# Moved time tables and two-part norm factors in a two-block transformer kernel

## The reference

```python
# block 1, gated linear attention: 4 heads, chunks of 64
log_a = log_sigmoid(g_lr @ w_gate2 + b_gate) / 16
b = cumsum(log_a)                       # inside a chunk
q_t, k_t = q * exp(b), k * exp(-b)
o = tril(q_t @ k_t.T) @ v + q_t @ state # state: a scan over kd = k * exp(b_last - b)
# block 1, compressed attention: 8 heads, the keys pooled into blocks
probs = softmax(mask(q @ k_cmp.T))
h = h + concat([o_nsa, o_gla]) @ w_out  # "half output": o_gla's half of w_out
# block 2
proj = rmsnorm(h) @ w_in
q, k = l2norm(silu(conv(dq))), l2norm(silu(conv(dk)))   # 8 heads of 128
g = -exp(a_log) * softplus(da + dt_bias)
beta = sigmoid(db)
o_dn = gated_delta_rule(q, k, v, g, beta)               # scan over chunks of 64
o_dn = rmsnorm(o_dn, dn_gain) * silu(dz)
qs, ks = rmsnorm(sq, sbq_gain), rmsnorm(sk, sbk_gain)   # stick-breaking attention
merged = sigmoid(gate_dn) * (o_dn @ w_dn) + sigmoid(gate_sb) * (o_sb @ w_sb)
```

## Time and profile before

| | before |
|---|---|
| median of 3 runs | 2299.69 us (2299.67 to 2304.11) |
| the profiled execution | 2297.21 us |
| its span | 2295.4 us |
| TensorE busy | 2198.8 us, 96% of the span |
| TensorE weight loads | 1700.5 us |
| VectorE busy | 1119.2 us, 49% |
| ScalarE busy | 804.2 us, 35% |
| DMA | 218.65 MB, mean 95 GB/s |

### The profile page before, as it was taken

How to read it: one execution, slowest core, us unless ns; L and a number is a source line. 1 busy time by engine, 2 the same in 40 slices (tenths; PEclk the granted TensorE clock), 3 DMA queues, 4 the chain that set the end, 5 groups by cost and what they waited for, 6 DMA issues and landing times. The chain is left out here.

```text
span 2295.4 us, 32701 instructions
## 1 busy us (share of the span) xinstructions
PE 2198.8 (96%) x13572; PEld 1700.5 (74%) x13572; DVE 1119.2 (49%) x1800; ACT 804.2 (35%) x1310; POOL 67.4 (3%) x88
## 2 busy tenths in 40 slices
PE   8999799999999899989998999998999999999999
PEld 7776456888888888977665888666566578888887
DVE  3464675777733467654345443346432254444422
ACT  3333554444422443422224222225345433222221
POOL 0000001000000000000000000000012101000000
PEclk8999899999999999989999999999999999999999
DMA  4124001322222244321114321114721322222322
GB/s 162 63 74 149 8 1 65 98 96 92 93 99 93 89 146 136 112 97 64 63 56 160 133 91 64 60 57 166 239 67 49 115 101 92 92 92 92 101 92 92
DMA packets 78595, 218.65 MB, mean 95 GB/s; under 512 B 8688, under 2 KB 13168, under 8 KB 78448
## 3 DMA queue, kind: packets, MB, share of 16 engines
q1 hardware_dynamic: 78448, 216.57, 28.1%
HBM read 185.74 MB, written 29.75 MB: 94 GB/s over the span
## 5 line engine op out<-in xcount | busy, mean ns | idle before, releaser
L296 PE MATMUL ps<-nx_hi,whi 128*128 128x264 f32 (+1 forms) x1504 | 538.1, 358 | 17.5 <-DVE nx_lo L385 9.7
L274 ACT ACTIVATE whi<-raw 128x1024 fp32r<-128x1024 f32 x282 | 298.4, 1058 | 625.4 <-PE ps L298 446.7
L281 DVE TENSOR_TENSOR wlo<-raw,whi 128x1024 fp32r<-128x1024 f32 x282 | 346.6, 1229 | 345.3 <-ACT whi L274 344.6
L298 PE MATMUL ps<-nx_hi,wlo 128*128 128x264 f32 (+1 forms) x1504 | 512.4, 341 | 0.0
L297 PE MATMUL ps<-nx_lo,whi 128*128 128x264 f32 (+1 forms) x1504 | 511.9, 340 | 0.0
L296 PEld LDWEIGHTS ps<-nx_hi,whi 128*128 128x128 f32 x1504 | 286.4, 190 | 85.0 <-issue 37.2
L298 PEld LDWEIGHTS ps<-nx_hi,wlo 128*128 128x128 f32 x1504 | 286.6, 191 | 32.6
L297 PEld LDWEIGHTS ps<-nx_lo,whi 128*128 128x128 f32 x1504 | 287.0, 191 | 30.4 <-issue 1.9
L298 PE MATMUL ps<-x_hi,wlo 128*128 128x512 f32 x528 | 209.6, 397 | 0.0
L297 PE MATMUL ps<-x_lo,whi 128*128 128x512 f32 x528 | 208.3, 395 | 0.0
L296 PE MATMUL ps<-x_hi,whi 128*128 128x512 f32 x528 | 208.0, 394 | 0.0
(11 more groups left out here) (460 smaller groups left out, 2868.8 us busy)
## 6 DMA issues: line engine op xcount, KB each, us to landing
raw<-stream_dram SPq DMA_DIRECT2D x285, 512.0 KB, 3.5
qk_spill<-ring SPq DMA_DIRECT2D x16, 264.0 KB, 2.1
qk_cols<-qk_spill SPq DMA_DIRECT2D x16, 264.0 KB, 4.1
v_spill<-ring SPq DMA_DIRECT2D x16, 264.0 KB, 2.2
v_cols<-v_spill SPq DMA_DIRECT2D x16, 264.0 KB, 4.5
dz_spill<-ring SPq DMA_DIRECT2D x16, 256.0 KB, 2.1
dz<-dz_spill SPq DMA_DIRECT2D x16, 256.0 KB, 5.1
sbk_spill<-ring SPq DMA_DIRECT2D x8, 264.0 KB, 2.1
```

The lines of the kernel that those rows point to most:

```text
L274: act.activation(K.whi[:, n % HL], K.raw[:, n % RAW], ACT.Copy).then_inc(K.s_hi, 1)
L281: dve.tensor_tensor(K.wlo[:, n % HL], K.raw[:, n % RAW], K.whi[:, n % HL].bitcast(F32), ALU.subtract).then_inc(K.s_lo, 1)
L296: pe.matmul(out, whi, xhi, start=start, stop=False, skip_group_check=skip)
L298: return pe.matmul(out, wlo, xhi, start=False, stop=stop, skip_group_check=skip)
```

## The change

Two kinds of things are changed. First, numbers in the time tables, and with them the order on the engines:

- `Gates`: sums on TensorE at 0.7 of the lane instead of 0.5, VectorE's copies at 0.8 (0.65), ScalarE's exponentials at 0.9 (0.8).
- `DeltaOutput`: the first unit's transposes from 0.43 on, 0.0125 for each block, instead of 0.36 and 0.025.
- `Linear`: cum 7.1 (6.6), kd_t 9.1 (8.6), states 10.3 (9.9), out 11.1 (10.9); log_a on VectorE at cum - 0.6 instead of cum - 0.2, which is a time of 6.5 instead of 6.4.
- `HalfOut`: from 1.0 to 7.4 instead of 0.5 to 6.5.
- `NormCols`: the last square four steps ahead of the first spread instead of two, the root 3.5 steps (1.5), the factors 3 steps (1); in its three stages the first square at 6.2 (5), 2.2 (1.0) and 1.0 (0.6), and a step of 0.18 (0.2) in the third.

Second, the spread of `NormCols`. The factors are kept in two fp32r parts, `rt_hi` and `rt_lo`, whose upper 64 rows are set to zero, and the identity in fp32r. A half is spread by two fp32r products on all 128 rows (hi and lo) in place of one fp32 product on its strip of 32 rows. ScalarE makes three more copies per stage, VectorE one more operation.

```diff
@@ HalfOut and the other time tables, one line of them
-                         HalfOut(K, o_hi, o_lo, (6, 7), z, 0.5, 6.5))
+                         HalfOut(K, o_hi, o_lo, (6, 7), z, 1.0, 7.4))
...
@@ class NormCols
+        self.rt_hi, self.rt_lo = [scratch(K, c, m, [P, HALF], F32R) for m in ("rt_hi", "rt_lo")]
+        self.ident = scratch(K, c, "ident_r", [P, P], F32R)
...
     def square_time(self, i):
         n = len(self.tiles)
-        return self.t0 + (self.spread_time(0) - 2 * self.step - self.t0) * i / n
+        return self.t0 + (self.spread_time(0) - 4 * self.step - self.t0) * i / n
...
             act.activation(self.sq[:, i % 2, 0:x.shape[1]], x, ACT.Square).then_inc(z["n_squares"], 1)
-        yield self.spread_time(0) - 1.5 * self.step
+            if i == 0:
+                none = cst(K, "ones")[64:P, 0:1].broadcast_to([64, HALF])
+                act.activation(self.rt_hi[64:P], none, ACT.Copy, scale=0.0)
+                act.activation(self.rt_lo[64:P], none, ACT.Copy, scale=0.0)
+                act.activation(self.ident[:], cst(K, "ident"), ACT.Copy).then_inc(z["n_ident"], 1)
+        yield self.spread_time(0) - 3.5 * self.step
...
             for h, (a, e) in enumerate(self.halves(x)):
-                mm = pe.matmul(K.ps[:, self.pairs[i % len(self.pairs)] + h, 0:e - a],
-                               cst(K, "ident")[32 * h:32 * h + 32, 32 * h + i:32 * h + i + 1].broadcast_to([32, P]),
-                               self.rt[32 * h:32 * h + 32, 0:e - a], start=True, stop=True)
+                out, row = K.ps[:, self.pairs[i % len(self.pairs)] + h, 0:e - a], self.ident[:, 32 * h + i:32 * h + i + 1].broadcast_to([P, P])
+                pe.matmul(out, row, self.rt_hi[:, 0:e - a], start=True, stop=False)
+                mm = pe.matmul(out, row, self.rt_lo[:, 0:e - a], start=False, stop=True)
             mm.then_inc(z["n_spread"], 1)
...
-        yield self.spread_time(0) - self.step
+        yield self.spread_time(0) - 3 * self.step
         dve.wait_ge(z["n_roots"], 1)
+        by = cst(K, self.scales, 64)
         K.dve_chain.link(dve, dve.reciprocal(self.rt[:], self.rt[:]))
-        dve.tensor_scalar(self.rt[:], self.rt[:], cst(K, self.scales, 64), None, ALU.mult).then_inc(z["n_factors"], 1)
+        K.dve_chain.link(dve, dve.tensor_scalar(self.rt_hi[0:64], self.rt[:], by, None, ALU.mult))
+        scaled_lo(dve, self.rt[:], by, self.rt_hi[0:64], self.rt_lo[0:64]).then_inc(z["n_factors"], 1)
```

More of the change, by code:

```diff
@@ L999, in pe @@
         pe.transpose(K.ps[0:META, 1, 0:16], abT[0:16, 0:META], ident[:, 0:16]).then_inc(z["gate_t"], 1)
-        yield self.at(0.5)
+        yield self.at(0.7)
         pe.wait_ge(z["gate_g"], 1)
@@ L1033, in dve @@
         dve.scalar_tensor_tensor(S.g[:, 32:40], xa[:, 32:40], -1.0, self.ea[:, 4:12], ALU.mult, ALU.mult).then_inc(z["gate_g"], 1)
-        yield self.at(0.65)
+        yield self.at(0.8)
         dve.wait_ge(z["gate_cum"], 1)
@@ L1051, in act @@
         act.activation(S.beta[:], self.bb[:], ACT.Sigmoid)
-        yield self.at(0.8)
+        yield self.at(0.9)
         act.wait_ge(z["gate_x"], 2)
@@ L1057, in act @@
         act.activation(S.egl.rearrange("p a b -> p (a b)"), K.ps[:, 4, 0:64], ACT.Exp).then_inc(z["gate_e"], 1)
-NORM_COL_SEMS = tuple(f"tile_in_{i}" for i in range(16)) + ("n_squares", "n_sums", "n_roots", "n_factors", "n_spread", "n_normed")
+NORM_COL_SEMS = tuple(f"tile_in_{i}" for i in range(16)) + ("n_ident", "n_squares", "n_sums", "n_roots", "n_factors", "n_spread", "n_normed")
 class NormCols(Lane):
@@ L1119, in pe @@
             if i == 0:
+                pe.wait_ge(z["n_ident"], 1)
                 pe.wait_ge(z["n_factors"], 1)
@@ L1693, in pe @@
                 u = 2 * j + f
-                yield self.unit(2 * u - 2) if u else self.at(0.36)
+                yield self.unit(2 * u - 2) if u else self.at(0.43)
                 if u >= 2:
@@ L1699, in pe @@
                         if m % 2 == 0:
-                            yield self.at(0.36 + 0.025 * m)
+                            yield self.at(0.43 + 0.0125 * m)
                         pe.wait_ge(z["o_normed"], m // 2 + 1)
@@ L2458, in dve @@
         dve.tensor_tensor(la[:], x4, bc(par(K, "b_gate"), [P, TT, 256], 1), ALU.add).then_inc(z["biased"], 1)
-        yield t_["cum"] - 0.2
+        yield t_["cum"] - 0.6
         dve.wait_ge(z["log_parts"], 1)
@@ L2978, in block1 @@
             rs = scratch(K, c2, "factor", [P, SEQ])
-            times = dict(logits=5.3, cum=6.6, kd_t=8.6, states=9.9, out=10.9, step=0.8, norm=14.6, o_t=16.4)
+            times = dict(logits=5.3, cum=7.1, kd_t=9.1, states=10.3, out=11.1, step=0.8, norm=14.6, o_t=16.4)
             linear = Linear(K, R, o_hi, o_lo, z, c2, (col, 5), (row, 4), (row, 8), times)
@@ L3051, in block2 @@
                          NormCols(K, [(S.qk[:, i], None) for i in range(8)], [(D2["qk1"], i) for i in range(8)], None, EPS,
-                                  "dn_scales", (0,), z, c3, 1.0, 8, 0.3),
+                                  "dn_scales", (0,), z, c3, 2.2, 8, 0.3),
                          dense, Lead(K, X, dense))
@@ L3080, in block2 @@
                                      [(D2["sbk"], i) for i in range(8)] + [(D2["sbq"], i) for i in range(8)], None, 128 * EPS,
-                                     "sb_scales", (2, 4), z, c3, 0.6, 8, 0.2),
+                                     "sb_scales", (2, 4), z, c3, 1.0, 8, 0.18),
                          ValueRows(K, v_rows, D2["sbv"], z, c3, 0, (z["n_roots"], 1), 5, 8),
```

2 lines of the change are left out of this document (1 added, 1 removed).

## The result

The changed kernel takes 2286.39 us (median of 6 runs, 2285.28 to 2287.57) where the kernel before takes 2303.98 (6 runs, 2299.67 to 2308.61) beside it: a ratio of 0.9927, with a 95% interval of 0.9913 to 0.9940. That is 17 us. The sum of terms was 17.7.

A forecast was written before the change was run, and what follows sets the result against it. TensorE, busy 96% of the span, was taken as the bound. Terms 4.2 - 4.5 + 3.8 + 7.9 + 0.7 + 5.6 = 17.7 off 2297.2 gave 2279.5, plus 2.5 for the median: 2282.0 us (range 2273 to 2291).

The forecast's parts named there:

- Linear attention, +4.2: Linear attention stage: more dense products ahead of the waits of 3.4 and 1.5, less new waits; 4.2 us gained.
- Compressed attention, -4.5: Compressed attention and half output: a split among the exponentials makes a new wait of 7.4; 4.5 us lost.
- Gates, +0.5: Gates' sums: the wait is renamed, 3.85 instead of 4.24, and the clock falls as before; 0.5 us gained.
- The factors, +1.4: Conv stage: factors come two steps earlier, half of the 2.7 wait is left; 1.4 us gained.
- the spread in the conv stage, +1.1: Conv stage: cheaper spread saves 2.8, of which about 1.7 returns as waits for VectorE; 1.1 us gained.
- The spread, 8.3 net: NormCols' spread in three stages: a tile costs 0.49 instead of 0.84, 11.2 over 32 tiles, 8.3 us net.
- Rival B: The spread saves nothing, the loss being in changing between kinds of product; tile stays 0.84, 2290.3 us; chance 0.20.
- First delta output, +7.9: First delta output: first square's wait falls from 7.3 to 4.8, later waits go, spread 2.0; 7.9 us gained.
- Second delta output, +0.7: Second delta output: first v_rows wait falls to 0.6, third pair waits 4.1; 0.7 us gained (-1 to +3).
- Second branch, +5.6: Second branch: first square's wait 0.7 becomes 0.3, and the spread gives 5.2; 5.6 us gained.

The follow-up runs named there:

- e_old_spread: Changed kernel with the old spread (one fp32 product per 32-row strip, no ScalarE copies), times as changed: 2291.93 us, ratio 0.9951 to the kernel before.
- e_tiles_first: Changed kernel with a column tile's load ahead of each dz load in the first delta output: 2288.45 us, ratio 0.9947 to the kernel before.
- e_early_square: Changed kernel, first delta output: tile loads from the start, dz later, first square ahead of the second rounding: 2285.78 us, ratio 0.9920 to the kernel before.
- e_norms_first: Changed kernel with VectorE's row norms in DeltaOutput 0.02 apart instead of 0.05: 2285.86 us, ratio 0.9931 to the kernel before.
- c_again: The changed kernel once more, nothing edited: 2286.37 us, ratio 0.9928 to the kernel before.
- e_half_back: Changed kernel with HalfOut at its old times (0.5 to 6.5): 2282.80 us, ratio 0.9909 to the kernel before.

## Why the prediction was right, point by point

The forecast was 2282.0 and faster; it is 2286.4, and 17 us against 17.7 where before and after are measured side by side. The difference of 4.4 is the reference: the median shown for before was of three runs, 2299.7, and over six it is 2304.0. That the whole comes within 1 us of 17.7 is partly luck. By stages the profiles miss their terms by 1.7, 1.6, 1.6, 0.7, 2.8 and 0.5, which cancel only in part, and their spans differ by 11.4; the medians give 17 because the profiled execution of before had lost less to the clock than its kernel mostly does.

- Linear attention, +4.2: waits of 0.6 and 0.7 instead of 3.4 and 1.5, as forecast, and the clock doesn't fall at 70. The stage gained 5.9 in the profile, 2.6 of it clock; by itself the change gives 3.5.
- Compressed attention, -4.5: the split among the exponentials makes TensorE wait 7.6 (forecast 7.4). 3.6 by the runs, 6.1 by the profile, of which 2.6 is clock.
- Gates, +0.5: the wait was renamed, 3.82 (3.85). The clock fell less than before in one execution (1.7, not 3.4) and as much in the other; in both it fell once more at 767 to 771, by 1.7.
- The factors, +1.4, and the spread in the conv stage, +1.1: waits of 1.6 and 1.5 as forecast. The stage made 2.2 instead of 3.8; the largest mis-sized term is the spread there, 1.1, of which VectorE's waits leave 0.2 (e_old_spread).
- The spread, 8.3 net: 5.6 and 7.3 by the two runs that change it alone. 0.47 a tile (0.49). Rival B was partly there: in the old unit the first products of the two strips start at 865.34 and 865.35, the second ones both at 865.67, and the next dense product at 865.98, so 0.64 of the 0.84 is products; the other 0.20 lies at the edges, whose steps are 0.21 and 0.23 instead of 0.12. The new unit has neither. The rival's reason, a small weight, isn't borne out: the strip's weight load took 0.18, a dense one's 0.19.
- First delta output, +7.9: 7.2. The wait was 5.7 (4.8), since the tile took 7.9 us to land and not 6.3. The step put the wait down to the tile's load, issued late, and in the changed kernel that load did end last. But it saw only half of the cause: a rounding that waits for its own chunk stands in front of the square and ends 0.2 us before, so with an early tile the wait is 6.5 (e_tiles_first), and with an early square it moves to another load (e_early_square).
- Second delta output, +0.7: the step that failed. Its own figures don't give +0.7: waits of 0.6 and 4.1 in place of 3.5 are 1.2 more, and no row shown accounts for the rest. The wait came as said, 3.9 (4.1), but I took the half clock behind it for what it was before. It was 1559 to 1567 instead of 1564 to 1569, and again 1593 to 1601 at the stage's end: -2.1, below the step's range of -1 to +3, with 2.1 of clock. e_norms_first takes the wait away and has the 3.4 back in that stage.
- Second branch, +5.6: 5.1.

Two rules of the Trainium skill bear on this. By TensorE: Matmul & The Clock Gate, Part 3: Packing small matmuls — row/col tiling, with four passes for true fp32 (FP8 and Floating Point Precision, TensorE Precision Notes), the old tile should have cost the 0.44 of an estimate, as the new one. The trace agrees that the two strips run side by side (starts 0.01 us apart). The new one does cost 0.47; the old one cost 0.84, and the measurement decides: 5.6 to 7.3 us over 32 tiles.

By the Trainium skill, TensorE: Matmul & The Clock Gate, Why this matters for your kernels, idle gaps over about 3 us cost the clock. All four waits of 3.8 and more were met or followed by a fall, as it says. But 2.68 brought one in one run and none in the next, in c_again there was one behind waits no longer than 1.9, and in every profile the one at the first delta rule behind 1.4. So with shorter gaps one isn't safe here; what the trace of before showed, 1.00 behind 2.7, was one case.

## What to carry to other kernels

When an order is moved to fill a wait, follow the releaser's own queue to its end: what ends each of the four long waits here stands behind a weight chunk's rounding or split on another engine. Small edits of such queues (gate functions, row norms, two copies ahead of the last weights) took 2 to 5 us off a wait each; in time none of them is clear of the noise by itself, but the three together, with HalfOut's old times, brought 15 us. Where the transfers of a stage are the limit, their order only chooses who waits. And compare sums over stages with the clock's share taken out: a clock that falls in one run and not in the next is worth more than most edits here (51.2 and 58.0 us lost by one kernel).

## What was not expected of the hardware

- The same kernel lost 51.2 and 58.0 us to half clock in two executions, with the same instructions; over the fourteen profiles the loss is 39 to 58. A fall lost 1.7, 3.4 or more, up to 11.9 in one (e_half_back, from 246 on).
- Two fp32 products on strips of 32 rows cost a tile 0.84, 0.20 of it at the change to and from dense products; four fp32r products on all 128 rows with a broadcast column as weights cost 0.47, at the spacing of dense products.
- In the first delta output a tile of 264 KB took 7.4 us to land (median of eight in e_tiles_first, the first of them 2.6) where the median over the whole run of before is 4.1.
